# Forgetting attention's turned probabilities: their trip to HBM and back moves from SyncE's line to GpSimd's queue

## The reference, cut to what matters

```python
def fox_attention(q, k, v, f_logit):
    c = jnp.cumsum(jax.nn.log_sigmoid(f_logit.astype(jnp.float32)), axis=1).transpose(0, 2, 1)
    ...
    def block(args):                      # one block of 128 queries
        qi, ci, blk = args
        s = jnp.einsum('bhqd,bkhd->bhqk', qi, k32) * scale
        s = s + ci[..., None] - c[:, :, None, :]
        s = jnp.where(kpos[None, :] <= qpos[:, None], s, -jnp.inf)
        p = jax.nn.softmax(s, axis=-1)
        return jnp.einsum('bhqk,bkhd->bqhd', p, v32)
```

## Time and profile before

| | |
|---|---|
| median of 3 runs | 1055.29 us (1054.19 to 1055.32) |
| the profiled execution: time, span | 1056.9 us, 1055.1 us |
| TensorE's granted clock | 0.999 of full speed |
| busy: PE, DVE, ACT, POOL | 1044.2, 755.5, 598.6, 71.0 us |
| DMA: SP's queue q1, POOL's queue q0 (share of 16 engines' span) | 67.6%, 3.1% |
| `fpT<-fp_turned`, 32 gathers of 48 KB: median from issue to landing | 3.5 us |
| `fp_turned<-fpT`, 8 stores of 192 KB: median from issue to landing | 2.1 us |

### The profile page before, as it was taken

One profiled execution on the slowest core, in us unless ns is written; L12 is line 12 of the kernel. 1 busy time (PEld: TensorE's weight loads), 2 busy tenths in 40 slices (PEclk: granted clock), 3 DMA queues, 4 the chain that ended last, 5 costly groups with the idle time before them and its releaser, 6 DMA issues.

```text
span 1055.1 us, 12945 instructions
## 1 busy us (share of the span) xinstructions
PE 1044.2 (99%) x4939; PEld 871.8 (83%) x4939; DVE 755.5 (72%) x901; ACT 598.6 (57%) x800; POOL 71.0 (7%) x59
## 2 busy tenths in 40 slices
PE   9999999999999999999999999999999999999997
PEld 7888888878888888888888888888879988888886
DVE  5768777776787676468997778868778666867642
ACT  6473767665384645448774645554366657565531
POOL 1200000000000000000434600000000000000000
PEclk9999999999999999999999999999999999999999
DMA  9945889896487787558857855889875346878751
GB/s 364 390 137 173 293 256 306 272 302 212 177 278 241 246 229 233 188 201 271 250 171 222 240 162 179 266 264 324 298 263 183 120 164 208 236 241 237 246 163 40
DMA packets 97645, 243.89 MB, mean 231 GB/s; under 512 B 15104, under 2 KB 41904, under 8 KB 97456
## 3 DMA queue, kind: packets, MB, share of 16 engines
q1 hardware_dynamic: 94016, 231.51, 67.6%
q0 software_dynamic: 3136, 11.23, 3.1%
q10 hardware_dynamic: 432, 0.33, 0.1%
HBM read 220.48 MB, written 22.54 MB: 230 GB/s over the span
## 4 chain that ended last, share of the span: by engine, by line
PE 76%; DMA 9%; DVE 7%; SPq 3%; issue 2%; ACT 2%; DVEq 0%; ACTq 0%
PE ps L820 17%; PE ps L822 17%; PE ps L821 17%; DMA gv_turned<-gv_blocked 5%; PE ps L857 5%; PE ps L859 5%; PE ps L858 5%; DVE rest L1964 2%; PE ps L954 1%; SPq L641 1%; DMA y_turned<-y_blocked 1%; PE ps L1144 1%; PE ps L1253 1%; PE ps L1255 1%; PE ps L1254 1%
## 5 line engine op out<-in xcount | busy, mean ns | idle before, releaser
L1964 DVE TENSOR_TENSOR rest<-raw,high 128x2048 fp32r<-128x2048 f32 x129 | 295.4, 2306 | 74.7 <-ACT high L1368 74.0
L820 PE MATMUL ps<-high,xt_high 128*128 128x512 f32 x824 | 324.6, 394 | 0.2 <-DVE rest L1964 0.2
L821 PE MATMUL ps<-rest,xt_high 128*128 128x512 f32 x824 | 321.0, 390 | 0.0
L822 PE MATMUL ps<-high,xt_rest 128*128 128x512 f32 x824 | 321.0, 390 | 0.0
L1368 ACT ACTIVATE high<-raw 128x2048 fp32r<-128x2048 f32 x129 | 244.3, 1910 | 68.6 <-DMA raw<-in_units_dram 68.5
L822 PEld LDWEIGHTS ps<-high,xt_rest 128*128 128x128 f32 x824 | 154.7, 188 | 32.3
L820 PEld LDWEIGHTS ps<-high,xt_high 128*128 128x128 f32 x824 | 154.9, 188 | 31.9 <-DVE rest L1964 0.6
L821 PEld LDWEIGHTS ps<-rest,xt_high 128*128 128x128 f32 x824 | 154.9, 188 | 30.9
L1969 DVE SCALAR_TENSOR_TENSOR rest<-raw,wgain,high 128x512 fp32r<-128x512 f32 x176 | 119.1, 746 | 35.7 <-ACT high L1372 35.7
L1372 ACT ACTIVATE high<-raw,wgain 128x512 fp32r<-128x512 f32 x176 | 110.9, 716 | 9.5 <-DMA raw<-in_units_dram 9.5
L1628 ACT ACTIVATE act<-ps,recips 128x256 f32<-128x256 f32 x44 | 18.4, 470 | 85.1 <-PE ps L822 85.0
(11 more groups left out here) (372 smaller groups left out, 1446.0 us busy)
## 6 DMA issues: line engine op xcount, KB each, us to landing
raw<-in_units_dram SPq DMA_DIRECT2D x350, 512.0 KB, 5.0
gv_turned<-gv_blocked SPq DMA_DIRECT2D x11, 512.0 KB, 7.9
gv_t<-gv_turned SPq DMA_DIRECT2D x44, 128.0 KB, 3.1
turned<-blocked SPq DMA_DIRECT2D x22, 256.0 KB, 5.3
hid_t<-turned SPq DMA_DIRECT2D x88, 64.0 KB, 4.1
fox_turned<-fqT SPq DMA_DIRECT2D x6, 512.0 KB, 3.3
raw<-in_units_dram SPq DMA_DIRECT2D x8, 256.0 KB, 4.4
fqT<-fox_turned SPq DMA_DIRECT2D x16, 128.0 KB, 4.2
```

Source lines behind the costliest of these rows:

```text
L820: pe.matmul(out, sh, wh, start=first, stop=False)
L821: pe.matmul(out, sh, wr, start=False, stop=False)
L822: mm = pe.matmul(out, sr, wh, start=False, stop=last)
L1964: vec.tensor_tensor(rest[:, slot, c], raw[:, slot, c], high[:, slot, c].bitcast(F32), ALU.subtract).then_inc(unit_rest, 1)
```

## The change

The store and the four gathers of every head leave SP's list. POOL issues them in a loop over the heads, after `differences(1)` and ahead of its waits for `oa_ready` and `fo` of head 7. The waits are the same two, on the same semaphores; the buffers, the number and the shapes of the transfers are the same. A head's store no longer waits for SP to come to a certain unit, and its gathers follow when the store has landed.

```diff
@@ load(u), on SyncE
                 turn_tokens(u)
-                turn_probabilities(u)
...
-            def turn_probabilities(u):
-                h = u - UNIT["win2"] - 33
-                if 0 <= h < HH:
-                    sync.wait_ge(fp_stored, 16 * (h + 1))
-                    src = fp_turned[h].rearrange("(q i) (r e) -> r i q e", q=4, r=4)
-                    for r in range(4):
-                        sync.dma_start(fpT[32 * r:32 * r + 32, h % 3, :].rearrange("p (q e) -> p q e", q=4), src[r]).then_inc(fp_landed[h % 3], 16)
-                h += 1
-                if 0 <= h < HH:
-                    sync.wait_ge(fp_blocked, h + 1)
-                    sync.dma_start(fp_turned[h], fpT[:, h % 3, :]).then_inc(fp_stored, 16)
@@ on GpSimd
+            def store_probabilities(h):
+                pool.wait_ge(fp_blocked, h + 1)
+                pool.dma_start(fp_turned[h], fpT[:, h % 3, :]).then_inc(fp_stored, 16)
+            def read_probabilities(h):
+                pool.wait_ge(fp_stored, 16 * (h + 1))
+                src = fp_turned[h].rearrange("(q i) (r e) -> r i q e", q=4, r=4)
+                for r in range(4):
+                    pool.dma_start(fpT[32 * r:32 * r + 32, h % 3, :].rearrange("p (q e) -> p q e", q=4), src[r]).then_inc(fp_landed[h % 3], 16)
             for n, name in enumerate(GAINS):
                 if name == "mem_kv":
                     clear_scores(0)
                     for hf in range(2):
                         differences(hf)
+                    for h in range(HH):
+                        store_probabilities(h)
+                        read_probabilities(h)
```

## The result

The changed kernel takes 1059.76 us in the median of 6 runs (1058.91 to 1062.43), the kernel before beside it 1055.14 (1054.19 to 1055.55, 6 runs). The ratio is 1.0047, with a 95% interval of 1.0037 to 1.0057: slower by 0.47%. The medians lie 4.6 us apart. The prediction was 1054.8 us, no change. The time lies inside the range, on the side that had 0.34, and it came about in the way of rival 1, which had 0.16. The profiled execution of the changed kernel took 1059.41 us, its span is 1057.6.

A forecast was written before the change was run, and what follows sets the result against it. PE was taken as the bound, busy 1044.2 of 1055.1 us. With POOL's turn (6.6 us) and trip (10.9 us) under their limits, only the 0.47 us stall goes: 1055.3 to 1054.8 us; range for all 1053.9 to 1061.

The forecast's parts named there:

- the side that had 0.34: Whole program: slower by more than 0.2% (2.1 us), nearly all of rival 1 and Rival 2 plus unseen costs, chance 0.34.
- rival 1: POOL's turn becomes the pace through weight-load traffic beside the store: +2.8 us (5.2 us store) to +13.2; chance 0.16.
- weight loads go out up to 6.2 us earlier. I cost that at nothing: SP's list, freed of 40 issues and 20.0 us of waits: earlier loads priced at zero, as PE waits for none.
- the store's term: A head's store on POOL's queue: 1.8 + 2.6 = 4.4 us to landing, bounds 3.1 and 7.8.
- The two rows of gains: Two 512 KB transfers on POOL's queue, 4.0 and 5.3 us, the difference put down to DVE being busy.
- The 1.3 us that I charged to a busy DVE: Transfers on POOL's queue: a busy DVE adds 1.3 us, besides 1.3 us for the queue.
- P: POOL's time on one head before the next: 4.4 + 0.1 + 2.1 = 6.6 us, limit 6.90.
- the margin of 0.3: POOL's turn per head: 6.6 us against heads coming every 6.90, so POOL keeps up by 0.3 us.
- The formula: PE's stalls by the last head: 7 x (P - 6.90) + (A - 11.9) us, first term only if P exceeds 6.90; less 0.47.
- A: One head's whole trip from transpose to use: 4.4 + 0.1 + 1.6 + 4.8 = 10.9 us, limit 11.9 at head 7.
- the stall: PE waiting at head 4 for its late gathers in the kernel before: 0.47 us, expected to be removed.
- Rival 2: DVE's 2.29 us rest operation holds back POOL's descriptors: store 5.3 us, +3.6 us, or +5.8 with gathers; chance 0.14.

The follow-up runs named there:

- thin loads: Changed kernel, but the ten weight units loaded in this stage load only 128 of 2048 columns, ScalarE and VectorE work as long as before; 1054.40 us, ratio 0.9994.
- the run with the memset: Changed kernel, but SP's weight load waits for a signal from a POOL memset placed behind the store's issue; 1054.70 us against 1055.29, ratio 0.9997.
- probabilities first: Kernel before, one line moved: in SP's line the probabilities' transfers come ahead of those of hg; 1054.52 us against 1055.26, ratio 0.9996.
- thin rests: Changed kernel, but for ten weight units DVE computes the rest of only 128 of 2048 columns, loads stay whole; 1057.78 us, ratio 1.0020.

## Why the prediction was wrong, step by step

**The step that failed is "weight loads go out up to 6.2 us earlier. I cost that at nothing".** It looked only at who waits for the loads, and there it was right: PE waits for no load. It didn't ask what an earlier load does to the transfer that it now comes ahead of. SP's waits for transposes, the 10.7 us that I read as slack, had been the timetable that kept 1 MB behind a 192 KB store. I knew of the load "less than 1 us ahead of the store" and made it rival 1, with 0.16; the price in the sum stayed without it. The same gap is in the store's term: 4.4 us started from SP's best landing, 1.8, with no load in it.

**The rows of before had the price, and I read them wrongly.** I set SP's slow stores aside "because SP's slow stores stood behind gathers in the same queue". The fast ones did too. Heads 2 and 5 of the kernel before, each with its landing:

```profile
655.10 2.19 SPq L663 DMA_DIRECT2D fpT<-fp_turned  x4
657.33 0.43 SPq L667 DMA_DIRECT2D fp_turned<-fpT  x1
...
DMA to landing us min/median/max: 2.0/2.0/2.0
...
675.23 2.07 SPq L663 DMA_DIRECT2D fpT<-fp_turned  x4
677.35 0.43 SPq L667 DMA_DIRECT2D fp_turned<-fpT  x1
...
DMA to landing us min/median/max: 6.5/6.5/6.5
```

What parts them is the weight load issued 4 to 6 us ahead: at 657.33 none is in flight, at 677.35 the one from 671.76 has 3.2 us to go. It is so for all eight. The stores of heads 3, 5 and 7 had 1.7 to 3.4 us of a load ahead of them and took 4.6, 6.5 and 4.3 us (with gathers of `hg` behind that load at heads 3 and 5); the other five had none, or 0.6 us, and took 1.8 to 2.1. The two rows of gains differ in this as well. At 283.99 no weight load was in flight, at 793.23 there was this one, its halves landing 3.8 and 4.6 us after issue:

```profile
791.64 0.80 SPq L603 DMA_DIRECT2D raw<-in_units_dram  x2
...
DMA to landing us min/median/max: 3.8/4.2/4.6
```

The 1.3 us that I charged to a busy DVE goes with a weight load issued 1.6 us ahead. No run took it away there, so for this transfer the load is the likely cause and not a shown one.

**The terms.** The store was 4.4 us in the sum and 4.9 on the chip. That they are near is luck: the 4.4 was 1.8 and two premiums, 1.3 for the queue and 1.3 for DVE. Measured, POOL's queue adds 0.3 us and a busy DVE nothing (thin loads: 2.1 us), and the load adds 2.8 at head 0 (4.98 - 2.15) and 2.5 in the mean (4.87 against 2.33 with thin loads). The last gather's landing, 4.8, was 5.0. The wake-up was 0.1 and is 0.3 (the landing at 647.48, the gathers at 647.77), four issues were 2.1 and are 2.2. P, over the seven full turns: 4.85 + 0.28 + 2.19 = 7.32, where I had 6.6 and the limit was 6.90. Even with my store, the two small terms would have used up nearly all of the margin of 0.3.

**The formula held, but for its last 0.47.** With P = 7.32 and head 7's A = 705.88 - 693.77 = 12.1 it gives 7 x 0.42 + 0.2 = 3.1 us, and 0.3 more because the first store starts 0.3 behind its transpose and not 0.03: 3.4, against the 3.5 measured from head 0 to head 7. I had taken off the 0.47 of the stall in each rival as well. That counts it twice: the 11.9 was read at head 7 of before, whose start already has that stall in it. Rival 1 would have stood at +3.3 for a 5.2 us store, and not at +2.8. The limit without the stall is also 11.4 and not 11.9 (701.56 - 690.14 in the run with the memset), so the forecast's margin at head 7 was 0.5 us and not 1.0.

**Right:** no head is held by POOL's other work, an issue is 0.55 us, and the stall was worth 0.47 us (probabilities first: 46.69 for 47.16). Also that rival 1 would show itself by stores that start later and later behind their transposes: head 0's by 0.3 us, head 4's by 3.2 and head 5's by 4.3; after head 5's store, which landed in 2.1 us, it is 2.9 and 2.4.

**Rival 2 is refuted** by thin loads and, from the other side, by thin rests. The Trainium skill (SBUF — State Buffer, Who interferes with whom) had said, as an inference, that a `tensor_tensor` doesn't hold GpSimd's descriptors back, and the runs agree: 2.1 us for the store with one beside it for 1.9 us. The Trainium skill (DMA: Bandwidth & Descriptors, Latency and other measured facts) gives first bytes from which the prediction took a premium of 0.4 us for GpSimd's path; by their landings the runs have 0.3.

**From the stage to the whole.** Span against span, the changed kernel is only 2.5 us longer than the profile of before (1057.6, 1055.1), but that profile has the 1.3 us wait at L857, which this one lacks. Against the version with the probabilities first (span 1053.0; its time is the same as before by its interval) it is 4.6 us longer: 0.4 up to head 0, 3.9 from head 0 to head 7 (50.63 - 46.69), 0.3 behind it. The first and last are within what equal kernels differ by: head 0 starts anywhere from 653.9 to 655.0 us in the others in which nothing holds it up, though nothing before it was edited.

**Open.** The packets show how the store is held up: head 0's take no more of the DMA engines when they are late (0.259 x 1.88 x 16 = 7.8 us in all) than when they are early (0.711 x 0.70 x 16 = 8.0 us in the run with the memset); they begin later, at about 645.7, when the load's first half lands. Why the engines serve the load first isn't shown. Nor is it known how small the lead may be. On POOL's queue 0.70 us ahead of the load is enough and 0.03 isn't, which fits with the descriptors being written during the 0.58 us of the issue, but nothing between the two was run.

## What to carry to other kernels

A wait in a line of transfers can be a timetable: before moving what it waits for to another queue, ask what large transfer the wait held back, and what small one on the critical path it will now go ahead of. Price a transfer at its landing beside the traffic that the change itself creates, taken from rows with that traffic, and not as a quiet landing plus a premium for the queue. When landings of one transfer spread from 1.8 to 6.5 us, look at each for the large transfer in flight at its issue, and how long that had to go, before the spread is put down to a queue or an engine. And where a chain of transfers in series is run by one engine, compare the whole turn with the pace of the work, each small wake-up and issue with it: here 0.4 us over the limit, seven turns in a row, cost more than the stall that the change removed.

## What the runs showed of the hardware

- A 192 KB store lands 1.8 us (SP) to 2.1 us (POOL) after issue, 5.0 us when a 1 MB load went out 0.85 us ahead of it, on either queue, and 5.6 us with the load 0.27 us ahead. 0.37 us (SP) and 0.72 us (POOL) ahead of the same load it takes 1.8 and 2.2. With half the load the median was 2.9. Issued with both halves of a load in flight and no transfer of `hg`, it lands 0.5 to 1.0 us after the second half in 22 of 24 cases (1.9 and 2.3 in the others).
- A semaphore that POOL's sequencer raises behind the issue of a transfer is there 0.03 us after that issue starts (heads 0 and 1), or up to 0.36 us before it starts where POOL is still at the issues ahead of it, and not when it ends 0.58 us later; one that an operation of POOL raises comes behind it.
- SP's load leaves 0.03 us after a transpose that both wait for, POOL's store 0.30 us after it.
- The last gathers of head 7 take POOL up to 1.27 us to issue, where all others take 0.55. Beside them DVE works on its gate:

```profile
700.14 2.36 DVE L2648 TENSOR_SCALAR gate<-gate 128x2048 f32<-128x2048 f32 x2
```

The Trainium skill (SBUF — State Buffer, Who interferes with whom) says that DVE's 2-port modes lock GpSimd out; these issues fit that. It hit two issues in the whole run and put head 7's last gather off by 0.7 us (its issue began 2.35 us after the first gather's, not 1.65). PE waits 0.98 us at that head; how much of it is owed to this isn't shown.
